# Output projections' norm in a two-layer decoder kernel: centre and weight in one VectorE operation, the root on ScalarE, the shift on GpSimd

## The reference, cut to what matters

```python
DN_ALPHA = (2 * DEPTH) ** 0.25
LN_EPS = 1e-5

def layer_norm(x, g, b):
    xf = x.astype(F32)
    mu = jnp.mean(xf, -1, keepdims=True)
    var = jnp.mean(jnp.square(xf - mu), -1, keepdims=True)
    return ((xf - mu) * lax.rsqrt(var + LN_EPS) * g + b).astype(x.dtype)

def reference(...):
    for i in range(DEPTH):
        y = gdn_mixer(...) if i % 2 == 0 else fox_mixer(...)   # each ends with "@ w_out"
        x = layer_norm(DN_ALPHA * x + y, ln_g[i], ln_b[i])
        gate = jax.nn.sigmoid((x @ ple_w_gate[i]).astype(F32))
        x = x + (gate * (p[i] @ ple_w_proj[i]).astype(F32)).astype(x.dtype)
    return x
```

## Time and profile before

| what | value |
|---|---|
| median of 3 runs | 1763.88 us (1763.09 to 1765.41) |
| the profiled execution: its own time | 1763.55 us |
| the profiled execution: its span, first to last instruction | 1761.8 us |
| PE busy | 1689.7 us, 96% of the span |
| DVE busy | 881.0 us, 50% |
| ACT busy | 789.0 us, 45% |
| POOL busy | 312.8 us, 18% |
| mean granted TensorE clock | 0.986 |

### The profile page before, as it was taken

How to read it: one execution, slowest core, us unless ns; L and a number is a source line. 1 busy time by engine, 2 the same in 40 slices (tenths; PEclk the granted TensorE clock), 3 DMA queues, 4 the chain that set the end, 5 groups by cost and what they waited for, 6 DMA issues and landing times. The chain is left out here.

```text
span 1761.8 us, 28773 instructions
## 1 busy us (share of the span) xinstructions
PE 1689.7 (96%) x11157; PEld 1289.0 (73%) x11157; DVE 881.0 (50%) x1655; ACT 789.0 (45%) x1288; POOL 312.8 (18%) x243
## 2 busy tenths in 40 slices
PE   9899999999999989889989999999999999899898
PEld 6777777777777767678777887666666666688686
DVE  5657566575766624854331200354444444577533
ACT  4646455474655632152222311565556565531411
POOL 5213212121321251300000000222221221013000
PEclk9999999999999999999989999999999999999999
DMA  6211020311101131051130201111111101051411
GB/s 158 45 42 37 25 49 14 60 37 25 49 13 38 60 97 61 24 167 46 39 110 13 84 2 41 44 38 39 46 34 43 43 22 43 1 172 44 143 46 51
DMA packets 115575, 94.42 MB, mean 54 GB/s; under 512 B 19761, under 2 KB 97777, under 8 KB 115441
## 3 DMA queue, kind: packets, MB, share of 16 engines
q1 hardware_dynamic: 115440, 92.59, 18.7%
HBM read 84.08 MB, written 8.49 MB: 53 GB/s over the span
## 5 line engine op out<-in xcount | busy, mean ns | idle before, releaser
L435 PE MATMUL gdn_unit<-part_hi,gdn_w_hi 128*128 128x512 f32 x496 | 226.4, 456 | 0.0
L437 PE MATMUL gdn_unit<-part_hi,gdn_w_lo 128*128 128x512 f32 x496 | 195.5, 394 | 0.0
L436 PE MATMUL gdn_unit<-part_lo,gdn_w_hi 128*128 128x512 f32 x496 | 194.5, 392 | 0.0
L2108 DVE CUSTOM_DVE_ANT_0 fa_probs<-fa_scores,fa_decay 128x896 f32<-128x896 f32 (+7 forms) x128 | 97.0, 758 | 121.0 <-PE fa_scores L1920 73.6
L867 DVE SCALAR_TENSOR_TENSOR x<-gdn_raw,gdn_taps,x 128x512 f32<-128x512 f32 x144 | 130.3, 905 | 31.4 <-ACT x L665 26.5
L399 POOL TENSOR_TENSOR gdn_w_lo<-ring,gdn_w_hi 128x1024 fp32r<-128x1024 f32 x31 | 75.5, 2435 | 238.5 <-ACT gdn_w_hi L645 238.5
L2054 ACT ACTIVATE fa_probs_t<-fa_turned 128x512 f32<-128x512 f32 (+1 forms) x96 | 52.3, 545 | 139.0 <-PE fa_turned L1937 138.5
L2048 ACT ACTIVATE fa_probs<-fa_probs,fa_top 128x896 f32<-128x896 f32 (+7 forms) x128 | 99.4, 777 | 22.1 <-DVE fa_top L2108 18.4
L437 PEld LDWEIGHTS gdn_unit<-part_hi,gdn_w_lo 128*128 128x128 f32 x496 | 93.4, 188 | 20.9
L435 PEld LDWEIGHTS gdn_unit<-part_hi,gdn_w_hi 128*128 128x128 f32 x496 | 94.0, 190 | 16.3 <-issue 3.9
L1295 PE MATMUL e_gate<-e_w_hi,part_hi 128*128 128x512 f32 x256 | 101.8, 398 | 2.9 <-DVE part_lo L1430 2.8
(11 more groups left out here) (329 smaller groups left out, 3681.4 us busy)
## 6 DMA issues: line engine op xcount, KB each, us to landing
ring<-in_gdn_w_in_dram SPq DMA_DIRECT2D x31, 512.0 KB, 4.1
ring<-in_ple_w_gate_dram SPq DMA_DIRECT2D x32, 256.0 KB, 3.0
ring<-in_fox_w_in_dram SPq DMA_DIRECT2D x32, 256.0 KB, 3.1
ring<-in_fox_w_in_dram SPq DMA_DIRECT2D x16, 512.0 KB, 4.8
fa_decay<-c_rows_scratch SPq DMA_DIRECT2D x64, 128.0 KB, 3.1
gdn_g_bc<-g_rows_scratch SPq DMA_DIRECT2D x8, 512.0 KB, 8.5
x_scratch<-x SPq DMA_DIRECT2D x8, 512.0 KB, 2.9
m_old<-x_scratch SPq DMA_DIRECT2D x8, 512.0 KB, 3.6
```

The costliest lines, as they stand in the source:

```text
L435: pe.matmul(out, w_hi[:, j % 2, k, :], xh[:, k, ts], start=(k == 0), stop=False)
L436: pe.matmul(out, w_hi[:, j % 2, k, :], xl[:, k, ts], start=False, stop=False)
L437: mm = pe.matmul(out, w_lo[:, j % 2, k, :], xh[:, k, ts], start=False, stop=(k == KT - 1))
L2108: step(dve.tensor_tensor_reduce(probs[:, n % 3, blocks(e)], scores[head][:, blocks(e)], decay[:, head, blocks(e)], 1.0, 3e38, ALU.add, ALU ...
```

## The change

For the turns 0 to 6 of both `mixer_out` phases, the order of the norm's factors is changed. VectorE no longer waits for `rstd`: one `scalar_tensor_tensor` subtracts the mean and multiplies by `gain`. ScalarE, after Ln and Exp, waits for that and multiplies the row tile by `rstd` in place (a Copy with the root as its scale), and GpSimd waits for ScalarE instead of VectorE before it adds `shift`. The last turn is as before.

```diff
+        rooted = sem("rooted")
...
                 step(act.activation(r, var, ACT.Ln, bias=eps[:, 0:1]))
                 step(act.activation(r, r, ACT.Exp, scale=-0.5), rstd_made)
+                if t < NT - 1:
+                    act.wait_ge(scaled, t + 1)
+                    step(act.activation(mixed[:, t % 2], mixed[:, t % 2], ACT.Copy, scale=r), rooted)
...
-                dve.wait_ge(rstd_made, i + 1)
-                step(dve.tensor_scalar(mixed[:, b], mixed[:, b], moments[:, b, 0:1], rstd[:, b:b + 1],
-                                       ALU.subtract, ALU.mult))
                 if i == 0:
                     dve.wait_ge(ln_loaded, 32)
-                step(dve.tensor_tensor(mixed[:, b], mixed[:, b], gain[:], ALU.mult), scaled)
+                step(dve.scalar_tensor_tensor(mixed[:, b], mixed[:, b], moments[:, b, 0:1], gain[:],
+                                              ALU.subtract, ALU.mult), scaled)
...
             for i in range(NT - 1):
-                pool.wait_ge(scaled, i + 1)
+                pool.wait_ge(rooted, i + 1)
                 step(pool.tensor_tensor(x1[:, turns[i]], mixed[:, i % 2], shift[:], ALU.add), x_made)
```

## The result

| what | before | with the change |
|---|---|---|
| median of 9 runs each | 1763.27 us (1763.09 to 1765.41) | 1768.32 us (1767.25 to 1769.91) |
| ratio | | 1.0026, 95% interval 1.0018 to 1.0035 |
| profiled execution, its span | 1763.55, 1761.8 us | 1768.52, 1766.8 us |

The change makes the kernel slower: its median is 5.05 us higher, and the ratio says 0.26%. That is over the 0.2% that a measurement can tell, though the interval reaches down to 0.18%. The forecast was 1767.9.

The account below looks back on a forecast made before the run. The prediction took m0 as a chain through VectorE and m1 as bound by PE. It summed 2.5 us for m0, 1.6 for the lower clock and 0.3 for the next phase to +4.4 on 1763.55: 1767.9 us, range 1767.0 to 1768.7.

Parts of the forecast that it names:

- What bounds m0 and m1: m1 belongs to PE, busy 91.2 of 94.6 us; m0 is a chain through VectorE, with PE waiting 3.9 us.
- Step 1: VectorE's two norm operations become one of 1.285 us that needs no root, by itself freeing 1.5 us a turn.
- Step 2: ScalarE gets a Copy of 128x1024 taking 1.15 us, starting 1.63 us after the start of the moments.
- Steps 3 and 4: High parts come behind the Copy, so VectorE's low part follows GpSimd's addition: mixes 0.12 us later before whole turns, 2.16 before short.
- the two bounds for the small low part: Mix before a short turn 3.55 us after the moments' start if not blocked by GpSimd's addition, 5.53 if blocked; blocked was taken.
- The sum for m0: PE's wait for turn 7 grows from 1.58 to 3.9 us; last moments at 752.05 against 749.54, +2.5 us.
- TensorE's clock: In m0, turn 7 runs at the lower clock after PE's longer wait: +1.6 us, bounds 0 and 1.6.
- The next phase: PE's pause before e0's flips shrinks from 5.43 to about 3.4 us, costing 0 to 0.9; 0.3 taken.
- the one without lower clock: Rival: the same chain in m0 without the 1.6 us in turn 7, 1766.3 us; chance 0.22.
- the one with an unblocked small low part: Rival: the small low part in m0 is not held by GpSimd's addition, 1762.1 us; chance 0.08.
- the faster one: Rival: low parts in m0 aren't held behind GpSimd's addition at all, -4.9 us, 1758.7 us; chance 0.06.

Follow-up runs that it names:

- e2: The kernel before with its old norm, but high and low parts for turn i + 3 ahead of the norm of turn i: 1757.45 us, ratio 0.9964.
- e7: The change with 20 small matmuls on constants ahead of PE's wait for turn 5 of m0 and 14 ahead of turn 7: 1767.26 us, ratio 1.0014.
- e1: The change, but ScalarE makes the high parts for turn i + 3 ahead of the multiplication by the root of turn i: 1754.01 us, ratio 0.9942.
- e3: The change without GpSimd's addition of the shift in turns 0 to 6, ScalarE's multiplication writing x1 itself: 1757.42 us, ratio 0.9969.
- e4: The change with GpSimd's addition made in two operations of 128x512 instead of one of 128x1024: 1764.44 us, ratio 1.0001.
- e5: The change with 28 small matmuls on constants ahead of PE's wait for turn 5 of m0 and 22 ahead of turn 7: 1766.93 us, ratio 1.0017.
- e8: The kernel before without GpSimd's addition of the shift in turns 0 to 6, VectorE's multiplication by gain writing x1: 1759.33 us, ratio 0.9974.

## Why the prediction was right, point by point

- **What bounds m0 and m1**: right. m1's length moved by 0.02 us, and VectorE's wait for the last product there grew from 3.5 to 4.0 us.
- **Step 1, VectorE's new operation**: 1.285 taken, 1.28 measured. Not seen: with no root to wait for in turn 0, VectorE came to the load of `gain` and `shift` earlier and stood 2.03 us for it. Where the phase begins at the full clock this reaches the path: the mix of turn 1 ran 14.37 us after the phase's start, and in e2, which also began so and waited for PE there, 13.85. That is 0.5 us, and 0.9 in e7.
- **Step 2, ScalarE's Copy**: 1.15 taken, 1.15 measured. It starts 1.62 us after the moments (1.63 said).
- **Steps 3 and 4, the low part always comes second**: right, and the term that decides, as e1 and e3 show. The small low part: mix 5.53 us after the moments said, 5.51 and 5.49 measured. The whole turn: 6.66 said, 6.57 measured. The choice between the two bounds for the small low part was settled by the trace: it is blocked, as the rule of the Trainium skill ("SBUF — State Buffer", "Who interferes with whom") has it. The 2.25 us for an operation of 0.29 agree with it, and so does the order of issue in e1.
- **The sum for m0**: PE's waits were 4.97 and 3.52 us (some 4.5 and 3.9 said). The last moments came 64.34 us after the phase's start against 61.36: +2.98 where the sum had +4.1. Of the 1.1 us too much, some 0.8 is the start of the phase, which the forecast took as unchanged ("that mix waits for PE"): in the change's profile PE had the full clock from the first matmul, VectorE didn't wait for it, and the mix of turn 1 ran 0.76 us sooner after the start. The rest is the 0.09 us per whole turn and the clock term. From the mix of turn 1 on, the change costs 3.74 us, so the chain itself was forecast to 0.4 us.
- **TensorE's clock**: 1.6 said, 1.45 measured by turn 7's length, 1.46 by e7.
- **The next phase**: the term that was mis-sized. PE's pause shrank to 3.40 us as said, but e0 cost 0.89 us up to its first tanh and 0.79 in its rest, against 0.3 for both. The shorter pause is not what cost it: e4 and e5 have the same pause (3.42 and 3.41 us) and took 28.71 and 28.70 us to the first tanh, against 28.60 before. What differs is where the lower clock falls, and nothing here shows that the change decides this. With m0 1.1 too long, the two errors nearly cancel: that the total of +4.4 is so close to +5.05 is in part luck. The clock's place at the start of a phase differs from profile to profile, so that a term of 0.3 us there could not have been read from one pair of phases.
- **The rivals**: the one without lower clock falls (0.60 behind turn 7's start); so does the one with an unblocked small low part, and the faster one. What that one described, low parts that are not held, is e3: 1757.42 against the 1758.7 worked out for it. Its profiled execution, though, took 1762.62, with m0 3.2 us shorter than before and not 4.9.

## What to carry to other kernels

Taking work off the late engine helps nobody if its next operand is made by the engine that got the work: put the operand that feeds TensorE first in that engine's order, the bookkeeping behind it. Where VectorE and GpSimd both read two SBUF tensors, look which of them starts first; coming second by 0.3 us turned 0.29 us into 2.25. And where TensorE waits for another engine, look at the granted clock behind the wait and count it as a part of the price: here it cost 1.46 us behind a wait of 3.52, and nothing behind one of 1.30.

## What had not been expected

- Two lines moved on ScalarE turn the change from 5.05 us slower into 9.3 us faster than before (ratio 0.9942, 0.9930 to 0.9955). Both the old and the new order had been paying the lock: 2 us in each whole turn of the old one, seen in e8.
- PE's waits of 1.14 (e8), 1.30 and 1.58 us were not followed by the lower clock, one of 1.80 us in e3 was. The length of a wait doesn't settle it alone: in e7 one of 2.21 us, with small matmuls ahead of it, was not followed by it either, and the pause of 3.4 us at the start of e0 was followed by a granted clock of 0.50 in e4 and of 1.00 in e3 and e7. A forecast that hangs on such a wait should carry both cases.
- The same code of e0 took between 28.6 and 30.2 us to its first tanh in eleven profiles, with the clock falling at different places of it: in the first 4 us the granted clock was 0.50 before and 1.00 in e3 and e7, and in the 4 us behind them 0.80 before and about 0.65 in those two.
